# A hybrid decoder trunk: the small loads of the beginning move from SyncE's queue to ScalarE's

## The reference

```python
cond = jax.nn.silu(c)
for i in range(DEPTH):
    mod = cond @ ada_w[i] + ada_b[i]
    sh1, sc1, g1, sh2, sc2, g2 = jnp.split(mod, 6, axis=-1)
    hm = modulate(x, norm_gain[i, 0], sh1, sc1)   # rms_norm(x, gain) * (1 + scale) + shift
    mix = ...                                     # attention, or the Mamba-2 mixer
    x = x + g1[:, None, :] * mix
    hf = modulate(x, norm_gain[i, 1], sh2, sc2)
    x = x + g2[:, None, :] * ffn                  # dense, or top 2 of 8 experts
```

## Time and profile before

| What | us |
|---|---|
| median of 3 runs | 1764.47 |
| lowest and highest run | 1763.08, 1766.15 |
| span of the profiled execution | 1763.7 |
| TensorE busy | 1675.2 (95%) |
| VectorE busy | 1447.0 (82%) |
| ScalarE busy | 1116.1 (63%) |
| data moved | 497.94 MB, mean 282 GB/s |

### The profile page before, as it was taken

One profiled execution on the slowest core, in us unless ns is written; L12 is line 12 of the kernel. 1 busy time (PEld: TensorE's weight loads), 2 busy tenths in 40 slices (PEclk: granted clock), 3 DMA queues, 4 the chain that ended last, 5 costly groups with the idle time before them and its releaser, 6 DMA issues.

```text
span 1763.7 us, 25287 instructions
## 1 busy us (share of the span) xinstructions
PE 1675.2 (95%) x7621; PEld 1328.8 (75%) x7621; DVE 1447.0 (82%) x1631; ACT 1116.1 (63%) x1357; POOL 0.2 (0%) x4
## 2 busy tenths in 40 slices
PE   7966999999998989899999999999999999999996
PEld 5632677777687777588888888888888888888884
DVE  5578687777547777599899899898998998998995
ACT  6343343443345584378778778777777787787773
POOL 0000000000000000000000000000000000000000
PEclk9987999999999998999999999999999999999998
DMA  8656498878354504189999999999999999999991
GB/s 341 215 177 220 136 371 284 283 273 282 109 204 131 191 1 142 49 303 365 334 371 369 343 356 375 334 366 344 379 353 334 384 357 337 367 367 335 365 374 73
DMA packets 206248, 497.94 MB, mean 282 GB/s; under 512 B 18188, under 2 KB 20541, under 8 KB 206025
## 3 DMA queue, kind: packets, MB, share of 16 engines
q1 hardware_dynamic: 206152, 496.91, 78.8%
HBM read 495.78 MB, written 1.07 MB: 282 GB/s over the span
## 4 chain that ended last, share of the span: by engine, by line
PE 84%; DVE 6%; issue 3%; ACT 2%; DVEq 0%; ACTq 0%
PE acc L1560 25%; PE acc L1567 24%; PE acc L1561 24%; PE xb L1839 2%; PE xb L1805 2%; PE acc L1545 1%; PE xb L1597 1%; DVE cv L1327 1%; PE acc L1933 1%; PE xb L1642 1%; PE acc L1663 1%; DVE w_lo L931 1%; PE xb L1828 1%; PE acc L1655 1%; DVE ada L958 1%
## 5 line engine op out<-in xcount | busy, mean ns | idle before, releaser
L931 DVE TENSOR_TENSOR w_lo<-raw,w_hi 128x1024 fp32r<-128x1024 f32 x848 | 1013.0, 1223 | 171.3 <-ACT w_hi L570 146.0
L570 ACT ACTIVATE w_hi<-raw 128x1024 fp32r<-128x1024 f32 x848 | 882.2, 1059 | 298.4 <-PE acc L1567 288.3
L1560 PE MATMUL acc<-w_hi,g_hi 128*128 128x512 f32 x896 | 354.3, 395 | 1.1 <-DVE g_lo L1506 1.1
L1561 PE MATMUL acc<-w_hi,g_lo 128*128 128x512 f32 x896 | 349.0, 390 | 0.0
L1567 PE MATMUL acc<-w_lo,g_hi 128*128 128x512 f32 x896 | 276.5, 390 | 0.1
L1567 PEld LDWEIGHTS acc<-w_lo,g_hi 128*128 128x128 f32 x896 | 168.1, 188 | 36.2 <-DVE w_lo L931 0.5
L1560 PEld LDWEIGHTS acc<-w_hi,g_hi 128*128 128x128 f32 x896 | 168.3, 188 | 34.6 <-issue 1.2
L1561 PEld LDWEIGHTS acc<-w_hi,g_lo 128*128 128x128 f32 x896 | 168.4, 188 | 33.2
L1560 PE MATMUL acc<-w_hi,a_hi 128*128 128x512 f32 x464 | 185.7, 400 | 6.0 <-DVE a_lo L981 4.5
L1561 PE MATMUL acc<-w_hi,a_lo 128*128 128x512 f32 x464 | 181.8, 392 | 0.0
L1560 PE MATMUL acc<-w_hi,e_hi 128*128 128x512 f32 x448 | 177.9, 397 | 0.0
(11 more groups left out here) (256 smaller groups left out, 1496.4 us busy)
## 6 DMA issues: line engine op xcount, KB each, us to landing
raw<-in_moe_w_gu SPq DMA_DIRECT2D x448, 512.0 KB, 6.0
raw<-in_moe_w_down SPq DMA_DIRECT2D x224, 512.0 KB, 5.3
raw<-in_ada_w SPq DMA_DIRECT2D x96, 512.0 KB, 5.5
raw<-in_ffn_w_gu SPq DMA_DIRECT2D x56, 512.0 KB, 5.5
raw<-in_ssm_w_in SPq DMA_DIRECT2D x40, 512.0 KB, 4.4
raw<-in_ffn_w_down SPq DMA_DIRECT2D x28, 512.0 KB, 5.0
raw<-in_ssm_w_out SPq DMA_DIRECT2D x16, 512.0 KB, 4.3
raw<-in_attn_w_qkv SPq DMA_DIRECT2D x12, 512.0 KB, 13.8
```

Of the source, the lines that this page charges most:

```text
L570: act.activation(w_hi[:, w % SPLIT, :], raw[:, no % RAW, :], ACT.Copy).then_inc(hi_ready, 1)
L931: dve.tensor_tensor(w_lo[:, w % SPLIT, :], raw[:, no % RAW, :], r32(w_hi[:, w % SPLIT, :]), ALU.subtract).then_inc(raw_used, 1)
L1560: pe.matmul(o, l_hi[:, k, rows_], hi[:, col:col + HALF], start=new, stop=False)
L1561: pe.matmul(o, l_lo[:, k, rows_], hi[:, col:col + HALF], start=False, stop=False)
```

## The change

Eleven of SyncE's thirteen small loads are now issued by ScalarE, ahead of its first computation. SyncE keeps `square` and `c` and goes on with the conditioning weights. `reversal`, which was second, now stands behind `x`. The second row of `norm_gain` (for the feed-forward norm of layer 0) is loaded after the last tile of `attn_w_qkv` and has a semaphore of its own; the waits on `ld_gain` are changed to fit.

```diff
             sp.dma_start(square[:, :, :], ...).then_inc(ld_square, 16)
-            sp.dma_start(reversal, square_in[:, 5 * P:6 * P]).then_inc(ld_square, 16)
             sp.dma_start(vec_rows[0:KD, :], A["c"]...).then_inc(ld_vecs, 16)
-            sp.dma_start(vec_rows[KD:KD + TAPS * CH, :], A["ssm_conv_w"]...).then_inc(ld_vecs, 16)
-            ...
-            sp.dma_start(x[:, :, :], ...).then_inc(ld_x, 16)
-            ...
-            sp.dma_start(qk_gain[:, 1, :], ...).then_inc(ld_att, 16)
...
                 if i == KD:
-                    for half in range(2):
-                        sp.dma_start(mod[:, 1 + 3 * half, :], row(A["norm_gain"][0, half:half + 1, :], D)).then_inc(ld_gain, 16)
+                    sp.dma_start(mod[:, 1, :], row(A["norm_gain"][0, 0:1, :], D)).then_inc(ld_gain, 16)
                     sp.wait_ge(xb_done[1], 1)
                     sp.dma_start(rel_dram, reltab[:, :]).then_inc(st_rel, 16)
...
+            sp.dma_start(mod[:, 4, :], row(A["norm_gain"][0, 1:2, :], D)).then_inc(ld_gain_ffn, 16)
             def bias_load(g):
...
         def _(act):
+            act.dma_start(vec_rows[KD:KD + TAPS * CH, :], A["ssm_conv_w"]...).then_inc(ld_vecs, 16)
+            act.dma_start(vec_rows[KD + TAPS * CH:P, :], A["ssm_conv_b"]...).then_inc(ld_vecs, 16)
+            act.dma_start(table[:, :], table_in).then_inc(ld_tab, 16)
+            act.dma_start(rel_rows[:, :], A["rel_bias"]).then_inc(ld_tab, 16)
+            act.dma_start(bias_rows[:, :], A["ada_b"]...).then_inc(ld_rows, 16)
+            act.dma_start(x[:, :, :], ...).then_inc(ld_x, 16)
+            act.dma_start(reversal, square_in[:, 5 * P:6 * P]).then_inc(ld_square, 16)
+            act.dma_start(w_r[:, :, :], ...).then_inc(ld_router, 16)
+            act.dma_start(sinks[:, :], ...).then_inc(ld_att, 16)
+            act.dma_start(qk_gain[:, 0, :], ...).then_inc(ld_att, 16)
+            act.dma_start(qk_gain[:, 1, :], ...).then_inc(ld_att, 16)
...
-                dve.wait_ge(ld_gain, 16 * 8)
+                dve.wait_ge(ld_gain, 16 * 7)
...
-                    dve.wait_ge(ld_gain, 32)
+                    dve.wait_ge(ld_gain if c == 1 else ld_gain_ffn, 16)
```

More of the change, by code:

```diff
@@ L233, in build @@
                          "ld_norm", "ld_router", "st_rel", "st_out"))
-    relb_set, cond_ready, ada_ready, ld_gain = (
-        sem(n) for n in ("relb_set", "cond_ready", "ada_ready", "ld_gain"))
+    relb_set, cond_ready, ada_ready, ld_gain, ld_gain_ffn = (
+        sem(n) for n in ("relb_set", "cond_ready", "ada_ready", "ld_gain", "ld_gain_ffn"))
     ss_ready, ms_ready, root_ready, hm_ready, x_ready = (
@@ L557, in _, with row @@
             steps = [0]
+            def row(src, n):
+                return bass.AP(src.tensor, src.offset, [[0, P], [1, n]])
+            act.dma_start(vec_rows[KD:KD + TAPS * CH, :], A["ssm_conv_w"][0].rearrange("t (k p) -> (t k) p", p=P)).then_inc(ld_vecs, 16)
+            act.dma_start(vec_rows[KD + TAPS * CH:P, :], A["ssm_conv_b"].rearrange("b (k p) -> (b k) p", p=P)).then_inc(ld_vecs, 16)
+            act.dma_start(table[:, :], table_in).then_inc(ld_tab, 16)
+            act.dma_start(rel_rows[:, :], A["rel_bias"]).then_inc(ld_tab, 16)
+            act.dma_start(bias_rows[:, :], A["ada_b"].rearrange("l (g n) -> (l g) n", n=D)).then_inc(ld_rows, 16)
+            act.dma_start(x[:, :, :], A["x"][0].rearrange("(t p) n -> p t n", p=P)).then_inc(ld_x, 16)
+            act.dma_start(reversal, square_in[:, 5 * P:6 * P]).then_inc(ld_square, 16)
+            act.dma_start(w_r[:, :, :], A["moe_w_router"][0].rearrange("(k p) n -> p k n", p=P)).then_inc(ld_router, 16)
+            act.dma_start(sinks[:, :], row(A["attn_sinks"], HEADS)).then_inc(ld_att, 16)
+            act.dma_start(qk_gain[:, 0, :], row(A["attn_q_gain"], HD)).then_inc(ld_att, 16)
+            act.dma_start(qk_gain[:, 1, :], row(A["attn_k_gain"], HD)).then_inc(ld_att, 16)
             def own(ins):
```

## The result

| | before | changed |
|---|---|---|
| median us | 1765.31 (4 runs) | 1773.87 (4 runs) |
| lowest to highest | 1763.08 to 1767.03 | 1771.85 to 1774.54 |
| span of the profiled execution | 1763.7 | 1772.7 |
| ratio, 95% interval | | 1.0045, 1.0033 to 1.0057 |

The change costs 7.9 us by the ratio (5.8 to 10.1); the medians differ by 8.6. The direction was forecast; the size, 4.45 us, was not, and the time lies above the stated range of 1764.3 to 1772.5.

The account below looks back on a forecast made before the run. TensorE bounds the kernel, so the first `w_hi` counts: it moves from 14.08 to 11.5 + 7.03 = 18.53, +6.9 for T less 2.48 of vanished waits. 1764.47 + 4.45 gives about 1768.9 us, range 1764.3 to 1772.5.

Parts of the forecast that it names:

- The bound, the beginning alone: Whole kernel: TensorE bounds it, so faster loads gain only at the beginning, through the first `w_hi` at 14.08.
- From the transpose to the first `w_hi`, 7.03 us: Beginning: ScalarE's own chain from TensorE's first transpose to the first `w_hi` takes 7.03 us without DMA waits.
- T: Start of TensorE's first transpose, which waits for `reversal` behind `x`: 11.5 us, between 8.2 and 14.5 at the widest.
- ScalarE's issues, 5.2 us: Start of ScalarE's queue: its 11 issues take about 5.2 us, from 0.73 to about 5.9, before its first table load.
- rival C: Beginning: two engines' issues wait for each other, T 13.5 to 14.5, +6.5 to +7.5 us, 1771 to 1772; chance 0.15.
- The lower bound, 13.75: Beginning: ScalarE's issues and table load alone put the first `w_hi` at 13.75, 0.3 us better than before.
- rival D: Beginning: faster, early tiles pay and `reversal` is no obstacle; -0.3 us, with the clock -2.0, 1762.5; chance 0.05.
- SyncE's wait for `reltab`: SyncE's queue after nine tiles: held from about 9 to 14.4 (T + 2.9), hidden by the backlog, cost nothing.
- The gain row: Moving 512 KB from behind the ninth tile brings the tenth 1.3 us forward; cost nothing, at most 0.4 us.
- The clock: TensorE's clock, conditioning and attention stages: taken as zero, with 1.7 us at each end and 1 us allowed for shifts.
- A: Beginning: the two queues do not hurt each other, T = 8.2, time 1764 to 1766, no change; chance 0.12.
- rival B: Beginning: coarse turns between queues (T = 10.7, +3.7 us) or a better clock (+2.8), 1767.3 to 1768.2; chance 0.18.

Follow-up runs that it names:

- `w_r` late: The changed kernel with `w_r` taken from ScalarE's list and issued by SyncE behind the `attn_w_qkv` tiles; 1772.05 us, ratio 1.0040.
- both edits: The changed kernel with `reversal` second in SyncE's queue and `w_r` issued by SyncE behind the `attn_w_qkv` tiles; 1765.63 us, ratio 1.0005.
- `reversal` first: The changed kernel with the load of `reversal` given back to SyncE, second in its queue behind `square`; 1768.68 us, ratio 1.0021.
- the tiles behind `x`: The changed kernel with SyncE waiting for `x` to land before it issues the first conditioning tile; 1765.72 us, ratio 1.0000.
- `x` first: The kernel with both edits, with `x` also moved to the front of ScalarE's queue; 1764.96 us, ratio 0.9996.

## Why the prediction was wrong

**The bound, the beginning alone: right in the main.** Of the 9.0 us by which the spans differ, 8.7 are there at the fillers, as the last paragraph of the prediction asked, and no wait for a DMA follows. (Of the waits of before, the prediction called two short: ScalarE's for `x` is, 0.4 us, but VectorE's for `rel_rows` is 4.0, and 7.3 in the changed kernel, off the path both times.) Later stages are not quite neutral, see the clock below.

**From the transpose to the first `w_hi`, 7.03 us: right.** 22.08 - 15.23 = 6.85, and with `w_r` late 21.95 - 15.09 = 6.86. No DMA wait is left in it.

**T, the landing of `reversal`: the step that failed.** It was put at 11.5, with 14.5 as the upper end, and came at 15.23. `x` was to land at 10.5: 8.0 for itself and 2.5 for a halved rate. It landed at 13.7. The halved rate is seen (130 packets to 127); what was missing is the time before it. I had let the small loads in front of `x` cost nothing extra, and they moved 0.11 MB in 4.5 us, with tiles on the other queue: the first 4 KB row came at 6.6 where it came at 3.8 without tiles. Those 2.8 us, and 0.3 for an issue of `x` at 3.02 instead of 2.70, are about the 3.2 by which `x` was late. `reversal` then paid its turns, 1.5 us behind `x`; the forecast had 1.3 for them and took 1.0. So the mechanism, shared engines and `reversal` behind `x`, was right, and the term was too small by 3.7 us, which is the miss in the total: 4.45 + 3.7 = 8.2 forecast with the right T, less 0.2 for the chain, 8.0 by the trace. The split of the 3.2 is read from single traces and is not a rule: with both edits the first 4 KB row came at 4.9, and `x` landed at 13.8 all the same.

**ScalarE's issues, 5.2 us: wrong, and hidden by the first error.** They took 13.0 (0.74 to 13.73). I had read the longer issues in SyncE's queue and kept them for rival C at the first issues, where they did not come; the hold came at the ninth, behind the 1024 pieces of `w_r`. That it can cost so much follows from the move: a held issue on SyncE delays transfers, on ScalarE it also delays all computing behind it. In the changed kernel this wait ends 0.7 us before the other, so even a right T would have met it: luck kept the 7.03 us of the chain intact. With `reversal` first it is the one that decides.

**The lower bound, 13.75, and rival D: not reached.** With both obstacles gone `x` itself is late (13.8), and the first `w_hi` at 16.4. The forecast had `x` in time for the squares. It was, at 13.7 instead of 10.5, only because the squares were late as well (19.57).

**SyncE's wait for `reltab`: right.** It ended at 18.17, at T + 2.9, and ScalarE had no wait for a tile afterwards. (The backlog was summed a little low: its 6.3 MB are 6.6 in the unit of the 416 GB/s, 16 us and not 15.)

**The gain row: right,** -0.5 (-2.1 to 1.1).

**The clock: not the cause, but not zero.** It did not stand at 2.4 GHz from the first tile. From the first tile to the fillers the changed kernel took 26.87 and 26.07 us in its two traces, against 26.14 to 26.24 before. The 0.7 us of the first is the low level that lasts to 28.46 there. In the attention stage the first trace loses 1.4 us more: its bias rows at 184.93 start 8.4 us after those of before and take 3.16 us instead of 1.98 at the low level, and the matmuls at 192.67 are 9.8 us later than theirs. The second trace has no such loss, 8.1 us at the fillers and 8.0 at 200 us. The forecast had allowed 1 us either way for this, as a guess.

**The rivals.** A, queues that do not hurt each other, is refuted by the tiles behind `x`: 5.6 us against 10.7. The rule that other issuers do not bring other DMA engines (the Trainium skill, "DMA: Bandwidth & Descriptors", section "Issuing engines are not separate DMA queues") is borne out by the same pair. The long turns of rival B, 9 to 17 descriptors in the Trainium skill's same page, section "Queues, rings and completion order", are not seen in the full stretches, where the two queues' counts agree to within one or two in each piece of 0.3 us. C gave the right size, 1771 to 1772, by the wrong way: ScalarE reached `x` at 3.02, 0.3 us later than forecast and not up to 2.4.

What stays open is the gap between the start and the time in three versions (`reversal` first, both, `x` first): their fillers are 5.2, 2.6 and 1.7 us behind the mean of before, their times 3.7, 0.9 and -0.7. In those traces the matmuls behind the second norm run at the 2.4 GHz level from the first one on; this is that stage in the kernel before and in the one with both edits:

```profile
484.84 0.63 PE L1561 MATMUL acc<-w_hi,a_lo 128*128 128x512 f32 x1
485.27 1.06 PE L1567 MATMUL acc<-w_lo,a_hi 128*128 128x512 f32 x2
```

```profile
486.55 0.40 PE L1564 MATMUL acc<-w_hi,a_hi 128*128 128x512 f32 x1
486.78 0.39 PE L1565 MATMUL acc<-w_hi,a_lo 128*128 128x512 f32 x1
```

0.63 us for a matmul against 0.40. The first matmul of that stage is 2.58 us behind the one of before (486.01, 483.43) and the transposes after it only 1.11 (488.84, 487.73): 1.5 us come back there. With `reversal` first and with `x` first 1.4 us more come back between the fillers and 200 us, and with both edits 0.8 us between 540 and 700 us. The traces of these three versions and of `w_r` late show the early level, the nine others do not. The size of the shift does not sort them: the stage begins at 484.04 and 491.57 in two that show it, at 483.82, 484.55 and 491.24 in three that do not. What does is open.

## What to carry to other kernels

A load that counts up a semaphore together with others is on the path of the first reader of that semaphore: before moving it, look who waits for the full count, and what stands ahead of it in its new queue. Issuing from a computing engine was cheap here only while its queue drained; with 1024 small pieces in it and tiles on the other queue it stopped the engine, and the DMA engines were shared anyway. If the first large load is late, take away what is ahead of it in the one queue (here -2.8 us) instead of opening a second (+7.9).

## What the runs showed of the hardware

- An issue can be held for many times its length by what is outstanding in the queue: 5.85 and 6.86 us for `sinks` with `w_r` ahead and tiles on the other queue; 0.47 without `w_r`; 0.61 with `w_r` but no tiles.
- Two full queues took turns one for one, whatever the size: 524 packets of one moved 1.92 MB and 526 of the other 0.02 MB in 5 us, and the counts agreed to within one or two in each of three pieces of 0.3 us.
- Small loads on one queue were held back by 4 KB rows on the other: 0.11 MB in the 4.5 us from 2.0, and the first 4 KB row behind them at 6.6 instead of 3.8.
- The scatter between executions begins in the first 15 us: the same first tile landed so that `w_hi` began at 13.53, 14.08, 14.55 and 15.29.
